# A layer norm between matrix products: apply its rows from PSUM with two VectorE steps per feature tile, and fill the TensorE pause

## The reference

```python
x = layer_norm(ALPHA * x + merged @ w_out, ln1_g, ln1_b)
u = causal_dwconv(x @ w_up, ffn_conv_w, ffn_conv_b)
gate, up = split(u)
f = (silu(gate) * up) @ w_down
x = layer_norm(ALPHA * x + f, ln2_g, ln2_b)

def layer_norm(x, g, b):      # over the 2048 features of each token
    mu = mean(x)
    var = mean((x - mu) ** 2)
    return (x - mu) * rsqrt(var + LN_EPS) * g + b
```

## Time and profile before

| | us |
|---|---|
| median of 3 runs | 2693.0 (2692.71 to 2695.34) |
| profiled execution, its own time | 2694.26 |
| its span in the trace | 2692.5 |
| PE busy | 2636.5 (98%) |
| DVE busy | 1781.0 (66%) |
| ACT busy | 1338.7 (50%) |
| POOL busy | 112.1 (4%) |

### The profile page before, as it was taken

One profiled execution on the slowest core, in us unless ns is written; L12 is line 12 of the kernel. 1 busy time (PEld: TensorE's weight loads), 2 busy tenths in 40 slices (PEclk: granted clock), 3 DMA queues, 4 the chain that ended last, 5 costly groups with the idle time before them and its releaser, 6 DMA issues.

```text
span 2692.5 us, 52683 instructions
## 1 busy us (share of the span) xinstructions
PE 2636.5 (98%) x22440; PEld 2588.5 (96%) x22440; DVE 1781.0 (66%) x2577; ACT 1338.7 (50%) x1811; POOL 112.1 (4%) x75
## 2 busy tenths in 40 slices
PE   8999999999999999999999999999899999999996
PEld 8998899899999999999899999999899999999996
DVE  6787779675555555566687786556676656665666
ACT  5474566454344443444445774444455435544543
POOL 2000021010000000000000000000400000000003
PEclk9999999999999999999999999999899999999998
DMA  6544445465555555555454555664365555555552
GB/s 243 179 149 141 172 150 191 146 205 195 192 194 196 195 191 195 196 193 177 165 171 151 167 190 193 195 195 165 127 205 194 196 195 193 193 195 194 193 193 87
DMA packets 136603, 488.44 MB, mean 181 GB/s; under 512 B 15153, under 2 KB 17585, under 8 KB 136369
## 3 DMA queue, kind: packets, MB, share of 16 engines
q1 hardware_dynamic: 136368, 485.09, 53.1%
HBM read 482.93 MB, written 2.10 MB: 180 GB/s over the span
## 4 chain that ended last, share of the span: by engine, by line
PE 92%; DVE 5%; ACT 1%; issue 1%; DMA 0%; SPq 0%; ACTq 0%; DVEq 0%
PE ps L794 91%; DVE WL L1760 2%; PE ps L797 1%; DVE XL L1768 1%; DVE xT L1760 1%; DVE T L1760 0%; DMA cst<-in_cst 0%; ACT P L1234 0%; ACT WH L1234 0%; ACT xT L1234 0%; DVE small L1768 0%; DVE P L1764 0%; DVE P L2041 0%; DVE small L1760 0%; DVE AL L1768 0%
## 5 line engine op out<-in xcount | busy, mean ns | idle before, releaser
L1760 DVE TENSOR_TENSOR WL<-raw,WH 128x1024 fp32r<-128x1024 f32 x907 | 1124.0, 1242 | 757.9 <-ACT WH L1234 757.5
L1234 ACT ACTIVATE WH<-raw 128x1024 fp32r<-128x1024 f32 x907 | 961.6, 1060 | 1281.6 <-PE ps L794 1278.1
L794 PE MATMUL ps<-XH,WH 128*128 128x256 f32 x5024 | 1403.4, 279 | 23.7 <-issue 10.8
L794 PE MATMUL ps<-XL,WH 128*128 128x256 f32 x5024 | 1392.0, 277 | 0.0
L794 PE MATMUL ps<-XH,WL 128*128 128x256 f32 x5024 | 1391.9, 277 | 0.0
L794 PEld LDWEIGHTS ps<-XH,WH 128*128 128x128 f32 x5024 | 945.8, 188 | 29.9 <-issue 26.5
L794 PEld LDWEIGHTS ps<-XL,WH 128*128 128x128 f32 x5024 | 945.7, 188 | 2.3 <-issue 1.5
L794 PEld LDWEIGHTS ps<-XH,WL 128*128 128x128 f32 x5024 | 945.4, 188 | 0.3
L794 PE MATMUL ps<-AH,WH 128*128 128x256 f32 x1856 | 513.1, 276 | 0.6 <-DVE AL L1760 0.4
L794 PE MATMUL ps<-AL,WH 128*128 128x256 f32 x1856 | 512.3, 276 | 0.0
L794 PE MATMUL ps<-AH,WL 128*128 128x256 f32 x1856 | 512.3, 276 | 0.0
(11 more groups left out here) (227 smaller groups left out, 1580.9 us busy)
## 6 DMA issues: line engine op xcount, KB each, us to landing
raw<-in_w_up SPq DMA_DIRECT2D x304, 512.0 KB, 4.3
raw<-in_w_in SPq DMA_DIRECT2D x224, 512.0 KB, 3.5
raw<-in_w_down SPq DMA_DIRECT2D x216, 512.0 KB, 3.5
raw<-in_w_out SPq DMA_DIRECT2D x64, 512.0 KB, 3.5
raw<-in_w_gates SPq DMA_DIRECT2D x64, 512.0 KB, 4.2
raw<-in_w_ckv SPq DMA_DIRECT2D x16, 512.0 KB, 3.2
raw<-in_w_cq SPq DMA_DIRECT2D x8, 512.0 KB, 4.2
raw<-in_w_co SPq DMA_DIRECT2D x8, 512.0 KB, 3.2
```

The lines of the kernel that those rows point to most:

```text
L794: return e.matmul(out, l, r, start=start, stop=True, skip_group_check=True)
L1234: return e.activation(out, x, func, **kw)
L1760: return e.tensor_tensor(out, a, b, op)
```

## The change

Both layer norms are rewritten in their last part, and the granule splits around the pause between `w_out2` and `w_gate2` are moved.

- `ln_s2`: the sums of x wait for `add2` or `add3` of their pair alone, and the sums of squares for `ln_sq`.
- `keep_busy`: after `ln_s2` PE runs four matmuls of a constant 128x128 matrix with 256 float32 columns, and after `ln_rows` of l = 0 three more; nobody reads the results.
- `ln_stat`: 17 instructions; three of them have no wait between them, nor have the two (one per half of the tokens) that make the variance.
- `ln_rowcopy` and POOL's `ln_scale_p` are gone. `ln_y` (DVE) does for each feature tile of 128x256 x * gain * root row, then shift row * gain + that, both `scalar_tensor_tensor` with the gain as a column, the rows read from PSUM. A pair takes four such instructions, a norm 32.
- l = 0: `ln_hi` (ACT, two of 128x256 per pair) adds the bias and writes `XH` from `ln_y`'s result; `ln_lo` (DVE, two per pair) writes `XL`. `ln_fin` (ACT, two per pair) adds the bias and writes `xT`, later. l = 1: `ln_fin` alone, then the store.
- Slots for l = 0: `ln_s2` X+3, `ln_stat` X+4, `ln_rows` X+5, `ln_y` of pair u X+6+u, `ln_hi` and `ln_lo` X+7+u, `ln_fin` X+9+u, and the pause is 7 slots in place of 11, so N is in slot X+8.
- `high(N+3)`, `low(N+2)` and `low(N+3)` move to slot X+3, ahead of `ln_stat`. `low(N+4)` to `low(N+8)` go one slot later than the rule (slot of the granule before), and `high` is as before from N+4 on: it leads the slot of the granule three before.

```diff
-PAUSE = {("w_co", 0, 0): 9, ("w_co", 0, 1): 1, ("w_gate2", 0, 0): 11}
+PAUSE = {("w_co", 0, 0): 9, ("w_co", 0, 1): 1, ("w_gate2", 0, 0): 7}
...
+        self.high_at, self.low_at = {}, {}
+        new = self.first["w_gate2", 0]
+        for g in range(4, len(self.grans)):
+            self.high_at.setdefault(self.slot[new - 1] + 3 if g == new + 3 else self.slot[g - 3], []).append(g)
+            early, late = g - new in (2, 3), 4 <= g - new <= 8
+            self.low_at.setdefault(self.slot[new - 1] + 3 if early else self.slot[g - 1 if late else g - 2], []).append(g)
...
-    for i, step in enumerate(("ln_s2", "ln_stat", "ln_rows", "ln_rowcopy")):
+    for i, step in enumerate(("ln_s2", "ln_stat", "ln_rows")):
         P.put(step, l, late + i)
-    P.B.book(("ln_s", l), s1, late + 3, "ln_rowcopy", l + 1)
-    P.T.book(("ln_row", l), late + 3, late + 12, "ln_move", 8 * l + 8)
-    out = []
+    P.B.book(("ln_s", l), s1, late + 10, "ln_y", 16 * l + 16)
     for u in range(8):
-        t = late + 4 + u
-        P.put("ln_scale_p" if u > 0 and (l == 0 or u % 2) else "ln_scale_v", (l, u), t)
-        P.put("ln_move", (l, u), t + 1)
-        P.put("ln_gain", (l, u), t + 2)
-        P.T.book(("ln_y", l, u), t, t + 2, "ln_gain", 8 * l + u + 1)
-        out.append(t + 2)
-    return out
+        t = late + 3 + u
+        end = t + 1 if l else t + 3
+        P.put("ln_y", (l, u), t)
+        if l == 0:
+            P.put("ln_hi", u, t + 1)
+            P.put("ln_lo", u, t + 1)
+        P.put("ln_fin", (l, u), end)
+        P.T.book(("ln_y", l, u), t, end, "ln_fin", 8 * l + u + 1)

 
 def make_plan():
...
                 for u in (6, 7):
-                    on.wait_ge(*s("ln_sq", 8 * l + u + 1))
+                    on.wait_ge(*(s("add2", u + 1) if l == 0 else s("add3", 17 + u)))
                     token_sums(out, 0, pair(xT, u), 2, False)
                 for u in (6, 7):
+                    on.wait_ge(*s("ln_sq", 8 * l + u + 1))
                     m = token_sums(out, 2, T("ln_sq", l, u), 2, False)
                 m.then_inc(s["ln_s2"], 1)
+                keep_busy(l, 4)
+            def keep_busy(l, n):
+                a, out = CL["ident"][0], bank(*(("w_down2", 10) if l else ("w_gate2", 0)), 0)
+                for _ in range(n):
+                    mm(out[:, 0:256], C("ones"), cst[:, a:a + 256])

             def ln_rows(l):
                 on.wait_ge(*s("ln_stat", l + 1))
                 for n, c in enumerate((8, 9, 10, 11)):
                     m = spread(S("ln_s", l)[:, 128 * n:128 * n + 128], stat[:, c:c + 1])
                 m.then_inc(s["ln_rows"], 1)
+                if l == 0:
+                    keep_busy(l, 3)
...
-            def ln_rowcopy(l):
-                free_T(on, "ln_row", l)
-                on.wait_ge(*s("ln_rows", l + 1))
-                fn(T("ln_row", l)[:, :], S("ln_s", l)[:, :], ACT.Copy).then_inc(s["ln_rowcopy"], 1)
-            def ln_gain(l, u):
-                y, g, b = T("ln_y", l, u), ("ln1_g", "ln2_g")[l], ("ln1_b", "ln2_b")[l]
-                on.wait_ge(*s("ln_move", 8 * l + u + 1))
+            def ln_hi(u):
+                y = T("ln_y", 0, u)
+                on.wait_ge(s["gemm"], P.count("w_out2", 3))
                 for n in range(2):
                     f = 2 * u + n
-                    m = fn(xT[:, f, :], y[:, 256 * n:256 * n + 256], ACT.Identity, scale=V(g, f), bias=V(b, f))
-                m.then_inc(s["ln_gain"], 1)
-            def f4_hi(u):
-                on.wait_ge(s["gemm"], P.count("w_out2", 3))
-                on.wait_ge(*s("ln_gain", u + 1))
-                fn(XH[:, 2 * u:2 * u + 2, :], xT[:, 2 * u:2 * u + 2, :], ACT.Copy).then_inc(s["f4_hi"], 1)
+                    on.wait_ge(*s("ln_y", f + 1))
+                    fn(XH[:, f, :], y[:, 256 * n:256 * n + 256], ACT.Identity, bias=V("ln1_b", f)).then_inc(s["ln_hi"], 1)
+            def ln_fin(l, u):
+                y = T("ln_y", l, u)
+                if l == 0:
+                    on.wait_ge(*s("ln_lo", u + 1))
+                for n in range(2):
+                    f = 2 * u + n
+                    on.wait_ge(*s("ln_y", 16 * l + f + 1))
+                    m = fn(xT[:, f, :], y[:, 256 * n:256 * n + 256], ACT.Identity, bias=V(("ln1_b", "ln2_b")[l], f))
+                m.then_inc(s["ln_fin"], 1)
...
-                if t in P.at and 4 <= P.at[t] + 3 < len(P.grans):
-                    high(P.at[t] + 3)
+                for g in P.high_at.get(t, ()):
+                    high(g)
...
-            def ln_scale_p(l, u):
-                free_T(on, "ln_y", l, u)
-                on.wait_ge(*s("ln_rowcopy", l + 1))
-                on.wait_ge(*s("ln_sq", 8 * l + u + 1))
-                e.tensor_tensor(two(T("ln_y", l, u)), xT[:, 2 * u:2 * u + 2, :], twice(T("ln_row", l)[:, 0:256]),
-                                ALU.mult).then_inc(s["ln_scale_p"], 1)
...
             def ln_stat(l):
                 x = S("ln_s", l)
-                d, v, rs, m = (stat[:, 4 + 2 * n:6 + 2 * n] for n in range(4))
+                d, v, rs, m, q = (stat[:, 4 + 2 * n:6 + 2 * n] for n in range(5))
                 on.wait_ge(*s("ln_s2", l + 1))
+                ts(q, x[:, 0:2], 1.0 / 2048, None, ALU.mult).then_inc(*own.up())
                 ts(d, x[:, 0:2], -1.0 / 2048, None, ALU.mult).then_inc(*own.up())
-                on.wait_ge(*own.now)
-                tt(v, d, d, ALU.mult).then_inc(*own.up())
-                on.wait_ge(*own.now)
-                stt(v, x[:, 2:4], 1.0 / 2048, v, ALU.mult, ALU.subtract).then_inc(*own.up())
-                on.wait_ge(*own.now)
-                rsqrt(rs, v, 2, 1.0, LN_EPS).then_inc(*own.up())
+                ts(m, x[:, 2:4], 1.0 / 2048, LN_EPS, ALU.mult, ALU.add).then_inc(*own.up())
+                on.wait_ge(*own.now)
+                for k in range(2):
+                    stt(v[:, k:k + 1], d[:, k:k + 1], q[:, k:k + 1], m[:, k:k + 1], ALU.mult, ALU.add).then_inc(*own.up())
+                root_of(rs, v, q).then_inc(*own.up())
                 on.wait_ge(*own.now)
                 tt(m, d, rs, ALU.mult).then_inc(s["ln_stat"], 1)

-            def ln_scale_v(l, u):
+            def ln_y(l, u):
+                g, rows, y = ("ln1_g", "ln2_g")[l], S("ln_s", l), halves_of(T("ln_y", l, u))
                 free_T(on, "ln_y", l, u)
-                on.wait_ge(*s("ln_rowcopy", l + 1))
-                tt(two(T("ln_y", l, u)), xT[:, 2 * u:2 * u + 2, :], twice(T("ln_row", l)[:, 0:256]),
-                   ALU.mult).then_inc(s["ln_scale_v"], 1)
-            def ln_move(l, u):
-                b = two(T("ln_y", l, u))
-                if u > 0 and (l == 0 or u % 2):
-                    on.wait_ge(*s("ln_scale_p", u if l == 0 else 8 + u // 2))
-                else:
-                    on.wait_ge(*s("ln_scale_v", 1 if l == 0 else 2 + u // 2))
-                tt(b, b, twice(T("ln_row", l)[:, 256:512]), ALU.add).then_inc(s["ln_move"], 1)
-            def f4_lo(u):
-                on.wait_ge(*s("f4_hi", u + 1))
-                pair_low(XH, XL, 2 * u, xT[:, 2 * u:2 * u + 2, :]).then_inc(s["f4_lo"], 1)
+                on.wait_ge(*s("ln_rows", l + 1))
+                done = []
+                for n in range(2):
+                    f = 2 * u + n
+                    stt(y[n], xT[:, f, :], V(g, f), rows[:, 0:256], ALU.mult, ALU.mult).then_inc(*own.up())
+                    done.append(own.now)
+                for n in range(2):
+                    f = 2 * u + n
+                    on.wait_ge(*done[n])
+                    stt(y[n], rows[:, 256:512], V(g, f), y[n], ALU.mult, ALU.add).then_inc(s["ln_y"], 1)
+            def ln_lo(u):
+                y = halves_of(T("ln_y", 0, u))
+                for n in range(2):
+                    f = 2 * u + n
+                    on.wait_ge(*s("ln_hi", f + 1))
+                    m = stt(XL[:, f, :], y[n], V("ln1_b", f), f32(XH[:, f, :]), ALU.add, ALU.subtract)
+                m.then_inc(s["ln_lo"], 1)
...
-                if t in P.at and 4 <= P.at[t] + 2 < len(P.grans):
-                    low(P.at[t] + 2)
+                for g in P.low_at.get(t, ()):
+                    low(g)
```

More of the change, by code:

```diff
@@ L62 @@
     "dn": "xbc_scale", "qi_rope": "qk_rope", "kw_ki": "dt_acs", "rq": "ssm_gain", "lru_la": "ssm_rs",
-    "lru_m": "rope_angle", "lru_scan": "rope_sin", "tk_start": "rope_cos", "gt_taps": "xr_taps", "f4_lo": "mg_lo",
+    "lru_m": "rope_angle", "lru_scan": "rope_sin", "tk_start": "rope_cos", "gt_taps": "xr_taps", "ln_lo": "mg_lo",
     "add3": "dn",
@@ L453, in make_plan @@
         P.chain(max([s for s, x in P.due["at_mul"].items() if u in x][0], E("att", 3)) + 1, u, ("mg_hi", "mg_lo"))
-    for u, t in enumerate(ln_steps(P, 0, "w_out2", 0, "add2", 0)):
-        P.put("f4_hi", u, t)
-        P.put("f4_lo", u, t + 1)
+    ln_steps(P, 0, "w_out2", 0, "add2", 0)
     for c in range(11):
@@ L782, in sync @@
                             lru_load(n)
-                for l, u in P("ln_gain", t):
+                for l, u in P("ln_fin", t):
```

(33 more changed lines are left out.)

2 lines of the change are left out of this document (1 added, 1 removed).

## The result

The changed kernel takes 2687.74 us (median of 20 runs, 2685.70 to 2691.70), the one before in the same session 2694.28 us (20 runs, 2690.98 to 2695.76). The ratio is 0.9979, with a 95% interval of 0.9973 to 0.9986. By the medians that is 6.5 us less, by the means 2694.06 - 2688.53 = 5.5 us. (± is one standard error.) Forecast were 3.6 us, so 2689.4, and a time between 2685.8 and 2693.2.

A forecast was written before the change was run, and what follows sets the result against it. PE's matmuls were taken to bound the kernel, with only its two layer-norm pauses movable. The tail's 2.2 us plus the first norm's 1.4 gave 3.6 us, so 2689.4 us against the median, range 2685.8 to 2693.2.

The forecast's parts named there:

- The deciding price: DVE in both norms: one `scalar_tensor_tensor` of 128x256 takes 0.393 us from start to start, bounds 0.31 and 0.476.
- The rival of the dearer DVE: Each DVE instruction with a PSUM operand costs its whole 0.476 us; the kernel gets slower, 2694.0 us; chance 0.13.
- The x sums: Last norm, PE: x sums start without waiting for the squares, and sums of squares end before the clock falls; 1.15 us saved.
- `ln_stat`: Last norm, DVE statistics: fewer waited steps, less a slower column operand, save 0.05 us, bounds 0 and 0.4.
- Rows and copy: Last norm, transposes to DVE's start: transposes stay at 1.12 us and dropping `ln_rowcopy` saves 0.75 us.
- Apply: End of the last norm: 32 DVE instructions plus ends take 13.3 us instead of 13.56, saving 0.26; last store unchanged.
- The first norm: Around the first norm: `gran(N)` starts 4.3 us earlier, but only 1.4 us is kept by granule N+8.
- the walk: Granules after the first norm, step by step: ACT's queue and 3.5 us DVE slots delay PE; N+8 at 1964.4, against 1965.9.
- the wait at N+3: PE after the first norm: pair 3 is ready 0.3 us late, so PE waits on `XL` at that granule.
- `keep_busy` at nothing: Constant matmuls in both norms: hidden under other work, too short to hold the clock, so worth no time.
- the clock is held: Rival: the constant matmuls keep PE at full clock through both norms; 7.0 us saved, 2686.0 us; chance 0.15.
- The queues eat the first norm's gain: Rival: `high(N+4)` ahead of `ln_hi` 2 and the DVE slots leave the first norm no gain; 2690.8 us; chance 0.12.

The follow-up runs named there:

- e5: The changed kernel with the norm's rows copied by ACT from PSUM to SBUF and read from there; 2693.32 us, ratio 0.9993.
- e4: The changed kernel with `ln_hi` issued ahead of `high` in each ACT slot; 2687.20 us, ratio 0.9972.
- e8: The changed kernel with `ln_hi` ahead of `high` in each ACT slot and without any constant matmuls; 2688.05 us, ratio 0.9976.
- e1: The changed kernel without the constant matmuls, nothing else changed; 2690.78 us, ratio 0.9986.
- e2: The kernel before the change with only the constant matmuls added, at the same two places; 2692.92 us, ratio 0.9997.
- e6: The kernel of e4 with three constant matmuls after `ln_s2` instead of four and five after `ln_rows` of the first norm instead of three; 2684.66 us, ratio 0.9965.
- e9: The same file as e6, run again on another chip; 2688.32 us, ratio 0.9976.

## Why the prediction came out as it did

The mechanism was right and most terms were too. The total was 1.7 us low by the means (3.6 against 5.3), but only 0.5 to 0.7 of that lies behind `add2`, where the change is. The time of one run could have moved by more than that with the clock alone: in the first series the twelve runs at 2685.70 to 2687.99 show a mean granted clock of 0.994, and the eight at 2689.57 to 2691.70 show 0.992 or 0.993.

- **The deciding price, 0.393 us**, measured 0.392, for all 32 in the last norm. The rival of the dearer DVE is out: the durations are 474 and 472 ns with a PSUM operand but the starts lie 0.392 us apart, and e5 shows the same spacing from SBUF. Everything that hung on the Trainium skill's figure for PSUM falls with it.
- **The x sums**, forecast 1.15 us: from `add3` to `ln_stat` it was 5.77 us and is 4.51, so 1.26. Of it 0.72 is the wait and 0.53 the clock, which in this execution fell behind the sums of squares (1.93 us against 2.46).
- **`ln_stat`**, forecast 0.05: start to transposes 3.16 and 3.10, so 0.06.
- **Rows and copy**, forecast 0.75: transposes to DVE's start 1.92 and 1.03, so 0.89. Of that 0.20 is the transposes, 0.92 us instead of 1.12: the filler brought the clock back in their midst. The copy alone gave 0.69.
- **Apply**, forecast 0.26: 16.03 and 15.64, so 0.39. Together 2.60 where the sum had 2.2.
- **The first norm**, forecast 1.4 and measured 1.52, by two errors that cancel, which was luck. `gran(N)` came 3.52 us earlier and not 4.3: the clock fell during the sums of squares (2.54 us, 0.5 more than before), and the filler ended at 1930.75, 0.34 us after `ln_stat`, so that the transposes queued behind it. In return the granules ran at half speed for 3.6 us and not 4.67. From there the walk held point by point: `high(N+4)` ahead of `ln_hi` 2, granules of 3.5 us at N+4 to N+6, and ACT's `high(N+11)` at 1962.29 where the forecast had N+8 at 1964.4, which less the 2.28 of the earlier start is 1962.1. e4 shows the place by moving it, and e8 against e1 shows it again. Only the wait at N+3 did not appear.
- **`keep_busy` at nothing** is the step that was mis-sized, on both sides. I took a constant matmul for at most 0.56 us at half clock, twice a transpose. It is two records of 0.445 us (eight in 3.56 us), where a transpose is one. The rows before had shown it: the eight calls of the x sums stand as x16. Four constant matmuls are 3.56 us and not 2.2, longer than `ln_stat`, and cost a third of a microsecond ahead of the rows of the first norm. And they are enough dense work to bring the clock back (1.00 from 1932.74), which I had excluded by calling them 1.1 us of work.
- **What the constant matmuls are worth.** By the times of e1 and e8 it is 1.7 ± 0.9 and 0.8 ± 0.75 us. Of that the traces show 0.2 us in the last transposes here (1.11 us in e1, 0.92 and 0.90 in two executions of the change, 0.71 in the third), and at most 0.5 (e2). In the first norm the half-speed stretch of the granules is 2.1 us shorter than in e1, worth 1.0 us, but `gran(N)` comes 0.84 us later. The pair e8 and e4, in which ACT's queue is out of the way, shows the same: 0.6 us gained behind `gran(N)`, 0.7 lost ahead of it. In both pairs most of the loss is the earlier fall of the clock among the sums of squares, ahead of the filler, and the filler's excess over `ln_stat` is the rest.
- **What stays open.** With the clock's fall in the sums of squares taken out (each last stretch less its sums' excess over 1.93 us), the last stretch is 26.35 us before, 24.28 after, 24.05 in e6, and 24.44 to 24.69 in e1, e4, e8 and e9: 1.7 to 2.3 us saved in each of them. The differences between executions of one kernel are mostly where the clock falls and rises, in the last norm (up to 1.6 us in the sums), and ahead of the first norm (up to 4.9 us over the same instructions, which no filler behind them can change). Whether the filler shifts the odds in the last norm, as the times of e1 and the change hint, or the series merely drew differently, these runs do not settle. Nor does a run take apart the rest of the change: the moved splits, the shorter pause and the new `ln_stat` were never undone one at a time, so their shares of the 3.52 us by which `gran(N)` came earlier are read from the trace and not tested.

Of the rivals, "the clock is held" did not happen in the change (0.50 over the first granules) but does with the filler of e6 and e9. "The queues eat the first norm's gain" is a real mechanism of some 2 us that did not eat all.

The version to take is e4, at 0.9972: the change with one loop moved. e6 and e9, one kernel, lie at 0.9965 and 0.9976, not distinguishable from it.

## What to carry to other kernels

When work is taken out of a pause, follow the in-order queues into the busy stretch behind it: here over half of what the first norm saved was given back, above all because an instruction whose input was ready stood behind one that waits for the engine being fed (e4: 1.96 us). Price an instruction by the distance from start to start in a row of the same form, not by its duration (0.392 us against 0.474). Size a filler by the records that the trace shows for one call, not by the calls. A gain of 0.2% needs the stretch measured in several traces, since the time of the whole kernel moves by as much with the place where the clock falls (4.9 us here, ahead of anything that was changed).

## What the runs showed of the hardware

- A 128x128 by 128x256 matmul of plain float32 shows as two records, and starts one every 0.445 us at the granted clock 0.50 (1.2 GHz). In the same trace and at the same clock an fp32r matmul of that shape is one record and starts every 0.213 us, so the plain one takes about four times as long.
- The clock (2.4 GHz to 1.2 GHz) falls at different places of the same instruction stream. In the last norm the 16 records of one-column sums of squares took 1.93, 2.46, 2.51, 3.03, 3.05 and 3.55 us in the executions of the change, the kernel before, e8, e9, e4 and e1, with PE busy throughout. Three executions of the change all had 1.93. Ahead of `add2` the same instructions had 3.4 to 13.7 us at granted clock 0.50, and ended up to 4.9 us apart.
- In the pause of the first norm the dense constant matmuls raised the granted clock to 1.00, and with 2.4 us of idle time behind them it was lost again just as the first granule began. With 0.4 us (e9) and 1.45 us (e6) it was kept.
- `scalar_tensor_tensor` of 128x256 float32 with a gain column: 0.392 us apart with a PSUM operand, 0.396 without, at durations of 472 to 479 ns.
